# A streamed mixture of experts with its weights in 4 MB transfers and four slots instead of 2 MB transfers and eight

## The reference

```python
h = rmsnorm(x);  proj = h @ w_in            # 2048 x 5376
y = concat(rg_lru(...), short_conv(...), stick_breaking_attention(...))
x = x + (per_head_rmsnorm(y) * mix_norm) @ w_out      # 2048 x 2048
h2 = rmsnorm(x)
# group = argmax of 4 logits, then the top 2 of the group's 8 experts
for e in the token's two experts:           # w_gate, w_up: 32 x 2048 x 512
    hid = silu(h2 @ w_gate[e]) * (h2 @ w_up[e])
    x = x + gate_e * (hid @ w_down[e])      # w_down: 32 x 512 x 2048
```

## Time and profile before

| | us |
|---|---|
| median of 3 runs | 1350.33 |
| lowest and highest | 1348.47, 1351.5 |
| span of the profiled execution | 1347.2 |
| the profiled execution's own time | not recorded apart from its span |

### The profile page before, as it was taken

How to read it: one execution, slowest core, us unless ns; L and a number is a source line. 1 busy time by engine, 2 the same in 40 slices (tenths; PEclk the granted TensorE clock), 3 DMA queues, 4 the chain that set the end, 5 groups by cost and what they waited for, 6 DMA issues and landing times.

```text
span 1347.2 us, 20449 instructions
## 1 busy us (share of the span) xinstructions
PE 1132.6 (84%) x8602; PEld 760.2 (56%) x8602; DVE 412.2 (31%) x700; ACT 308.0 (23%) x534; POOL 51.0 (4%) x64
## 2 busy tenths in 40 slices
PE   8999999999999878769778966976796697779676
PEld 7999999999985445226333522633352252335223
DVE  6545666675443333003101300300130030013002
ACT  6445576684430100000000000000100000010000
POOL 1110011501000000000000000000000000000000
PEclk9999999999999888779776877977887798779768
DMA  9954554745668999999999999999999999999995
GB/s 314 283 187 139 174 166 148 243 133 185 254 248 323 423 422 421 419 420 420 424 423 423 423 423 420 420 422 423 423 423 423 422 418 420 422 425 422 423 422 236
DMA packets 120306, 471.64 MB, mean 350 GB/s; under 512 B 8547, under 2 KB 69569, under 8 KB 103361
## 3 DMA queue, kind: packets, MB, share of 16 engines
q1 hardware_dynamic: 120256, 470.94, 87.8%
HBM read 468.83 MB, written 2.10 MB: 350 GB/s over the span
## 4 chain that ended last, share of the span: by engine, by line
PE 48%; DMA 41%; SPq 5%; DVE 2%; ACT 2%; issue 1%; DVEq 0%; ACTq 0%
PE bank L1316 24%; DMA ring<-in_w_up 22%; DMA ring<-in_w_down 14%; PE bank L1531 6%; DMA ring<-in_w_gate 5%; SPq L372 5%; PE bank L1482 5%; PE bank L1495 4%; PE bank L1563 3%; PE bank L1546 3%; PE bank L1268 1%; PE bank L1335 1%; DMA x_acc<-in_x 1%; PE bank L1367 0%; PE bank L1439 0%
## 5 line engine op out<-in xcount | busy, mean ns | idle before, releaser
L1531 PE MATMUL bank<-ring,x_exp 128*32 128x512 f32 x2048 | 298.3, 720 | 151.5 <-DMA ring<-in_w_up 104.8
L1531 PEld LDWEIGHTS bank<-ring,x_exp 128*32 128x32 f32 x2048 | 63.0, 121 | 356.3 <-DMA ring<-in_w_up 152.1
L865 DVE TENSOR_TENSOR w_lo<-ring,w_hi 128x1024 fp32r<-128x1024 f32 x116 | 145.4, 1271 | 141.5 <-ACT w_hi L549 141.4
L1563 PE MATMUL bank<-ring,hidT 128*32 128x256 f32 x2048 | 169.9, 501 | 22.0 <-DVE hidT L1223 21.2
L1316 PE MATMUL bank<-hT_hi,w_hi 128*128 128x256 f32 x576 | 164.7, 286 | 1.8 <-DVE hT_lo L836 1.8
L1316 PE MATMUL bank<-hT_hi,w_lo 128*128 128x256 f32 x576 | 163.0, 283 | 0.0
L1316 PE MATMUL bank<-hT_lo,w_hi 128*128 128x256 f32 x576 | 163.0, 283 | 0.0
L549 ACT ACTIVATE w_hi<-ring 128x1024 fp32r<-128x1024 f32 x116 | 121.8, 1059 | 134.7 <-PE bank L1316 134.7
L1218 DVE COPY up_sb<-bank 128x512 f32<-128x512 f32 x32 | 22.1, 692 | 396.2 <-PE bank L1531 396.2
L1563 PEld LDWEIGHTS bank<-ring,hidT 128*32 128x32 f32 x2048 | 84.5, 143 | 96.2 <-issue 77.2
L1316 PEld LDWEIGHTS bank<-hT_hi,w_hi 128*128 128x128 f32 x576 | 110.5, 192 | 2.2 <-issue 2.0
(11 more groups left out here) (229 smaller groups left out, 1163.2 us busy)
## 6 DMA issues: line engine op xcount, KB each, us to landing
ring<-in_w_gate SPq DMA_DIRECT2D x64, 2048.0 KB, 27.3
ring<-in_w_up SPq DMA_DIRECT2D x64, 2048.0 KB, 25.0
ring<-in_w_down SPq DMA_DIRECT2D x64, 2048.0 KB, 34.6
ring<-in_w_in SPq DMA_DIRECT2D x21, 2048.0 KB, 9.1
ring<-in_w_out SPq DMA_DIRECT2D x8, 2048.0 KB, 8.3
x_acc<-in_x SPq DMA_DIRECT2D x4, 1024.0 KB, 8.6
out<-x_acc SPq DMA_DIRECT2D x8, 256.0 KB, 2.2
lru_w<-in_lru_wa SPq DMA_DIRECT2D x1, 384.0 KB, 3.8
```

The costliest lines, as they stand in the source:

```text
L865: dve.tensor_tensor(w_lo[:, k].rearrange("p c n -> p (c n)"), src, w_hi[:, k].rearrange("p c n -> p (c n)").bitcast(F32), ALU.subtract).th ...
L1531: ins = pe.matmul(dst[SLOTS * j:SLOTS * (j + 1), :], x_exp[:, c, cols], weights[:, cc * F:(cc + 1) * F], start=(c < 4), stop=(c >= KC - 4))
L1563: ins = pe.matmul(b_down[h][SLOTS * n:SLOTS * (n + 1), 0:DB], hidT[:, f, :], weights[:, f * (D // 2) + n * DB:f * (D // 2) + (n + 1) * DB] ...
```

## The change

- `PARTS` goes from 6 to 3: whole gate, whole up, whole down, one transfer of 4 MB each. Every one is a single run of 32 KB in each partition.
- The experts' ring is `twin`, four slots of 4 MB over the same memory, in the order of old slots 6+7, 2+3, 0+1, 4+5. Its semaphores are its own. Each slot is released when the whole matrix is used.
- TensorE multiplies a whole matrix between two waits. The number of gate and up matmuls is the same; down is 16 matmuls with 512 columns instead of 32 with 256.
- The down product needs one bank. It is copied out once after the whole of it, 512 columns in each copy, and `combine` waits for that.
- Quad 0 gathers all four blocks and transposes the gates ahead of its first item, as the other quads do.

```diff
@@ -55,7 +55,7 @@
 
     PW = 256
     PIECE = KC * PW * 4
-    MIX_RING, MOE_RING = 4, 8
+    MIX_RING, MOE_RING = 4, 4
 
     BLK_XA, BLK_GA, BLK_BG = 0, HA, 2 * HA
     BLK_CG, BLK_XB = BLK_BG + HB, BLK_BG + 2 * HB
@@ -72,14 +72,13 @@
     Y_ORDER = (3, 0, 1, 2)
 
 
...
     QI = 4
     QUADS = NE // QI
     XQ = 4
     NX = XQ * QI
     NI = NE + NX + QI
-    H = KC // 2
 
     x_t = x[0].rearrange("(t p) d -> t p d", p=P)
     out_t = out[0].rearrange("(t p) d -> t p d", p=P)
@@ -104,7 +103,8 @@
         w_lo = at("w_lo", [4, 4, PW], F32R, 5 * PIECE)
 
         ring_at = [i * PIECE for i in range(6)] + [o_proj + 16 * SEQ * 4 + i * PIECE for i in range(2)]
-        ring = [at(f"ring{i}", [KC * PW], F32, ring_at[i]) for i in range(MOE_RING)]
+        ring = [at(f"ring{i}", [KC * PW], F32, ring_at[i]) for i in range(MIX_RING)]
+        twin = [at(f"twin{i}", [2 * KC * PW], F32, ring_at[i]) for i in (6, 2, 0, 4)]
         o = 6 * PIECE
         x_acc = at("x_acc", [TILES, D], F32, o)
...
@@ -198,13 +198,14 @@
         AUX = 4
 
         b_gate, b_up, b_fold = bank[0], bank[1], bank[2]
-        b_down = [bank[3], bank[4]]
+        b_down = bank[3]
         b_gath, b_comb = [bank[4], bank[5]], [bank[6], bank[7]]
 
 
         x_in, par_in, router_in = [sem(f"x_in{t}") for t in range(TILES)], sem("par_in"), sem("router_in")
         lru_in, x_again, out_done = sem("lru_in"), sem("x_again"), sem("out_done")
...
@@ -248,25 +249,21 @@
         give_full, give_ready = sem("give_full"), sem("give_ready")
 
 
-        MOE_ORDER = [6, 7] + [(N_MIX + i) % MIX_RING for i in range(MIX_RING)] + [4, 5]
-        MIX_USES = [len(range(i, N_MIX, MIX_RING)) for i in range(MIX_RING)] + [0] * 4
         PER_QUAD = PARTS * QI
         assert PER_QUAD % MOE_RING == 0
 
         def place_of(k, i):
 
-            return MOE_ORDER[(PARTS * k + i) % MOE_RING]
+            return (PARTS * k + i) % MOE_RING
 
         def piece_count(q, k, i):
 
-            rounds = (PARTS * k + i) // MOE_RING + 1 + MIX_USES[place_of(k, i)]
+            rounds = (PARTS * k + i) // MOE_RING + 1
             return q * (16 * PER_QUAD // MOE_RING) + 16 * rounds
 
 
         def piece_source(i, e):
-            if i < 4:
-                return (w_gate_p, w_up_p)[i % 2][e][:, (i // 2) * H:(i // 2 + 1) * H, :]
-            return w_down_p[e][:, :, (i - 4) * (D // 2):(i - 3) * (D // 2)]
+            return (w_gate_p, w_up_p, w_down_p)[i][e]
 
         def out_block(b):
 
...
@@ -355,13 +352,13 @@
                 def item_pieces(k, e):
                     for i in range(PARTS):
                         m = PARTS * k + i
-                        if isinstance(q, int) and m < 2:
+                        if isinstance(q, int) and m == 0:
 
                             sp.wait_ge(y_split, 4)
-                        elif isinstance(q, int) and m < 6:
-
-                            sp.wait_ge(lo_ready, 4 * (N_MIX - 6 + m) + 4)
-                        elif isinstance(q, int) and m < 8:
+                        elif isinstance(q, int) and m < 3:
+
+                            sp.wait_ge(lo_ready, 4 * (N_MIX - 3 + m) + 4)
+                        elif isinstance(q, int) and m == 3:
 
                             sp.wait_ge(quarter_used, 4 * N_MIX)
                         else:
@@ -369,8 +366,8 @@
                             sp.wait_ge(piece_used, q * PER_QUAD + (m - MOE_RING + 1))
                         place = place_of(k, i)
                         src = piece_source(i, e)
-                        sp.dma_start(ring[place][:, :].rearrange("p (c n) -> p c n", n=src.shape[2]),
-                                     src).then_inc(piece_in[place], 16)
+                        sp.dma_start(twin[place][:, :].rearrange("p (c n) -> p c n", n=src.shape[2]),
+                                     src).then_inc(twin_in[place], 16)
 
                 for k in range(QI):
...
@@ -746,7 +743,7 @@
             def item_step(q, k):
                 i = q * QI + k
 
-                act.wait_ge(piece_used, i * PARTS + 3)
+                act.wait_ge(piece_used, i * PARTS + 1)
                 if not (isinstance(q, int) and i == 0):
                     act.wait_ge(fold_full, i)
                 act.activation(gate_sb[:, :], b_gate[:, :], ACT.Copy).then_inc(gate_out, 1)
@@ -757,11 +754,10 @@
                 act.activation(silu_sb[:, :, :], b_fold[:, 0:P].rearrange("p (f s) -> p f s", f=FC),
                                ACT.Silu).then_inc(silu_ready, 1)
 
-                for h in range(2):
-                    act.wait_ge(piece_used, i * PARTS + (5 + h))
-                    for n in range(2):
-                        ins = act.activation(y_cols(k, h, n), b_down[h][SLOTS * n:SLOTS * (n + 1), 0:DB], ACT.Copy)
-                    ins.then_inc(y_out_act, 1)
+                act.wait_ge(piece_used, i * PARTS + 3)
+                for n in range(2):
+                    ins = act.activation(y_cols(k, n), b_down[SLOTS * n:SLOTS * (n + 1), :], ACT.Copy)
+                ins.then_inc(y_out_act, 1)
 
             def quad(q, n_extra=None):
...
@@ -1194,7 +1190,7 @@
                 for b in range(4):
                     dve.wait_ge(gath_full, q * 4 + (b + 1))
                     if not isinstance(q, int) and b == 0:
-                        dve.wait_ge(piece_used, q * PER_QUAD - 2)
+                        dve.wait_ge(piece_used, q * PER_QUAD - 1)
                     dve.tensor_tensor(x_exp[:, 4 * b:4 * b + 4, :],
                                       b_gath[b % 2][:, :].rearrange("p (c s) -> p c s", c=4),
...
@@ -1224,11 +1220,10 @@
                                   b_fold[:, P:2 * P].rearrange("p (f s) -> p f s", f=FC),
                                   ALU.mult).then_inc(hid_ready, 1)
 
-                for h in range(2):
-                    dve.wait_ge(piece_used, i * PARTS + (5 + h))
-                    for n in range(2, 4):
-                        ins = dve.tensor_copy(y_cols(k, h, n), b_down[h][SLOTS * n:SLOTS * (n + 1), 0:DB])
-                    ins.then_inc(y_out_dve, 1)
+                dve.wait_ge(piece_used, i * PARTS + 3)
+                for n in range(2, 4):
...
@@ -1467,10 +1462,10 @@
             keep_clock(bank[0], 10)
 
 
-            def outputs_written(q, k, h):
-
-                pe.wait_ge(y_out_act, q * (2 * QI) + (2 * k + h + 1))
-                pe.wait_ge(y_out_dve, q * (2 * QI) + (2 * k + h + 1))
+            def outputs_written(i):
+
...
@@ -1512,24 +1507,19 @@
                 first = isinstance(q, int) and i == 0
                 cols = slice(SLOTS * k, SLOTS * (k + 1))
 
-                for p in range(4):
-                    if first and p == 2:
-
-                        gather(q, range(2, 4))
-                        transpose_gates(q)
-                    weights = ring[place_of(k, p)]
-                    pe.wait_ge(piece_in[place_of(k, p)], piece_count(q, k, p))
-                    dst = (b_gate, b_up)[p % 2]
-                    if p < 2 and not first:
+                for p in range(2):
+                    weights = twin[place_of(k, p)]
+                    pe.wait_ge(twin_in[place_of(k, p)], piece_count(q, k, p))
+                    dst = (b_gate, b_up)[p]
+                    if not first:
                         pe.wait_ge((gate_out, up_out)[p], i)
-                    for cc in range(H):
-                        c = (p // 2) * H + cc
+                    for c in range(KC):
                         j = c % 4
-                        if k == 0 and p % 2 == 0 and j == 0:
+                        if k == 0 and p == 0 and j == 0:
 
                             pe.wait_ge(gath_out, q * 4 + (c // 4 + 1))
                         ins = pe.matmul(dst[SLOTS * j:SLOTS * (j + 1), :], x_exp[:, c, cols],
-                                        weights[:, cc * F:(cc + 1) * F], start=(c < 4), stop=(c >= KC - 4))
+                                        weights[:, c * F:(c + 1) * F], start=(c < 4), stop=(c >= KC - 4))
                     ins.then_inc(piece_used, 1)
                 if k == QI - 1:
                     keep_clock(bank[5], 5)
@@ -1551,33 +1541,26 @@
                     keep_clock(bank[5], 6)
 
                 pe.wait_ge(hid_ready, i + 1)
-                for h in range(2):
-                    if not first:
-
-                        pe.wait_ge(y_out_act, q * (2 * QI) + (2 * k + h - 1))
-                        pe.wait_ge(y_out_dve, q * (2 * QI) + (2 * k + h - 1))
-                    weights = ring[place_of(k, 4 + h)]
-                    pe.wait_ge(piece_in[place_of(k, 4 + h)], piece_count(q, k, 4 + h))
-                    for f in range(FC):
-                        for n in range(4):
-                            ins = pe.matmul(b_down[h][SLOTS * n:SLOTS * (n + 1), 0:DB], hidT[:, f, :],
-                                            weights[:, f * (D // 2) + n * DB:f * (D // 2) + (n + 1) * DB],
-                                            start=(f == 0), stop=(f == FC - 1))
-                    ins.then_inc(piece_used, 1)
```

(30 more changed lines are left out.)

11 lines of the change are left out of this document (7 added, 4 removed).

## The result

| | before | changed |
|---|---|---|
| median, us | 1349.49 (4 runs, 1348.47 to 1351.50) | 1338.83 (4 runs, 1338.73 to 1339.32) |
| span of the profiled execution | 1347.2 | 1337.0 |
| mean granted clock | 0.875 | 0.883 |

What follows compares the result with a forecast made beforehand. The prediction took transfers to bound the experts' stage. Run length -18.7, start +5.8 and end +5.0 sum to -7.9 us, from 1350.33 to 1342.4, with a range of 1336 to 1352.

Steps and rivals of the forecast that it cites:

- What bounds the kernel: Experts' stage: transfers set the pace (DMA share 1.01 at 422 GB/s) and TensorE follows; the mixer's stage is TensorE's.
- Run length: Experts' stream: fewer, longer runs bring every 4 MB matrix to 9.73 us; over 91 matrices -18.7 us.
- The start: First refill: it waits for the whole gather and all of gate, so it goes out later, +5.8 us.
- The end: After the last up lands: more matmuls on up, partly at lower clock, and `combine` waiting for copies, +5.0 us.
- Hidden work: Other items and quad boundaries: later releases cost nothing; worst release 36.7 us after up's landing, 10 us to spare.
- The rival of a dry ring: Between quads: the ring empties if TensorE is 10 us later than worked out; +30 us, 1372; chance 0.05.
- gate and up gain nothing: Gate and up transfers: no gain from longer runs, down only reaches their pace; -1.5 us, 1348.8; chance 0.17.
- down is slow for its place: Down's transfers: slow for following up while TensorE folds, so pace stays; +10.8 us, 1361; chance 0.05.
- its weaker form: Down's transfers: two fifths of the extra are its runs', the rest its place; +3.3 us, 1353.6; chance 0.08.

Runs made afterwards that it cites:

- down16: Kernel before, with each down piece cut by rows, one run of 16 KB instead of four of 4 KB: median 1336.86 us, ratio 0.9888.
- runs16: Changed kernel with two of its four slots split into two 16 KB stretches, still one transfer per matrix: median 1342.84 us, ratio 0.9933.
- two_dmas: Changed kernel with each matrix fetched by two transfers of 2 MB (16 KB runs): median 1345.78 us, ratio 0.9953.
- cols: Changed kernel with the down product in halves of the columns, each half copied out while the next is multiplied: median 1339.57 us, ratio 0.9913.
- best: Changed kernel with the edits of early, cols and up_half together: median 1332.95 us, ratio 0.9859.
- best2: best without the six idle matmuls between fold and down: median 1333.94 us, ratio 0.9878.
- late8: Changed kernel with 29 idle matmuls ahead of the gather of quads 1 to 7: median 1342.82 us (two executions), ratio 0.9935.
- again: The changed kernel itself, measured once more on the same chip as edits of its end: median 1339.92 us, ratio 0.9918.
- early: Changed kernel with the first item in halves as before and the two first refills cut in half: median 1335.0 us, ratio 0.9878.
- up_half: Changed kernel with the last up of each quad in two transfers of 2 MB: median 1336.37 us, ratio 0.9897.
- no_spin: Changed kernel without the six idle matmuls between fold and down of each quad's last item: median 1339.38 us, ratio 0.9916.

## Why the prediction held, step by step

**What bounds the kernel** held: in every run above the span ends 27 to 34 us after the last up has landed, so that this landing and the work behind it are the time.

**Run length** held. Down's excess goes with the way it is cut (down16), and going from 16 to 32 KB brings 9.5 ns a run (runs16, two_dmas) where 8.5 had been carried over from down. Beyond 16 KB the length of the runs is shown to be the cause, since runs16 changes nothing in the stream but that and where in a partition the halves lie. Between 4 and 16 KB the strided source is a second difference which no run takes away; that the two prices are nearly the same speaks for the runs there too. The forecast's 9.73 us was 9.715. By the traces the pace accounts for 30 x (10.21 - 9.715) + 61 x (9.80 - 9.715) = 20.0 us of the 22.1; the forecast had 18.7. The remaining 2 us are no pace. Of these 1.1 are in a stretch of the trace before, which the forecast read past, since it took its pace from 604.49 on and its stretch from 410.35. TensorE's timeline there is this:

```profile
573.59 3.64 PE L1531 MATMUL bank<-ring,x_exp 128*32 128x512 f32 x16 [1.27 <-DMA ring<-in_w_up]
...
589.94 1.92 PE L1531 MATMUL bank<-ring,x_exp 128*32 128x512 f32 x16 [0.70 <-DMA ring<-in_w_gate]
594.68 3.24 PE L1531 MATMUL bank<-ring,x_exp 128*32 128x512 f32 x16 [2.82 <-DMA ring<-in_w_up]
```

From the second half of up to the next item's first half are 21.09 us, where the same four pieces take 20.01 in the earlier trace rows. Another 0.4 us is lost between 453.94 and 469.45. The traces of cols, best, best2 and late8 have such losses of 1.0 to 2.7 us as well; those of the changed kernel, again, early, down16, two_dmas, runs16, up_half and no_spin have none above 0.3 us past 453 us. Over all their executions runs16 stays within 0.9 us, two_dmas within 1.4 and the changed kernel within 0.6 and later 1.6, the kernel before within 5.8. What causes these losses stays open, and so does whether the change has a part in their being rarer.

The Trainium skill's price of about 3 cycles per packet ("DMA: Bandwidth & Descriptors", "Why small descriptors are slow") would be 3.5 ns at the fabric clock that the Trainium skill gives there. The runs show 8.5 ns between 4 and 16 KB and 9.5 between 16 and 32 KB: it names the right cost and under a half of its size. The Trainium skill's fabric ceiling of 435 GB/s (same page, "Specifications") agrees: 4.194304 MB in 9.715 us are 432 GB/s, just below it.

**The start** held: 5.5 us for 5.8, and early takes all of it back.

**The end** was mis-sized, 6.3 us for 5.0. Of the parts, up at a clock between the two levels was right (5.15 us against the 1.92 of before, 3.2 for 3.5) and so nearly were the copies (1.8 for 1.5). What the sum left out is that the idle matmuls between fold and down can run at the lower clock as well (2.91 us for 12 records, 1.58 at full clock in up_half) and hold down back by 2.0 us, where it was 0.7. Also, the 26.9 us that it started from were an end at full clock: in the trace before, up, the idle matmuls and down were all granted 1.00. That the range of 3.3 to 6.8 holds the 6.3 is in part luck: in again the end costs 7.5 us, with up at 6.34 and down at 5.01, a term for which the sum had nothing. In down16 an end of 33.0 us stands behind a last up of half the size. So what the end costs depends on the clock at least as much as on the large slots; only up_half's medians, 2.5 to 3.6 us lower, show the slots' own part.

**Hidden work** held: 36.8 us to the release for 36.7, and about 9 us of room for 10. The forecast took one boundary for all of them, though; at the first the release comes after 42.8 us and the room is 2 to 3. The rival of a dry ring is real, but at the other boundaries it begins only where TensorE is 8 to 9 us later.

**The rivals.** That gate and up gain nothing is refuted by two_dmas and runs16. That down is slow for its place is refuted by down16, in its weaker form too: all of the 0.21 us a piece went.

The total was nearer than its parts. The stream gave 3.4 us more than forecast, the start cost 0.3 less and the end 1.3 more.

## What to carry to other kernels

A stream that is bound by its transfers gets faster with longer runs, and these do not need large slots: down16 had 15.4 of the stream's 22.1 us with the old ring, by cutting one matrix along the other axis, and its median was not above the changed kernel's. What large slots cost is paid once, where the ring is full before the consumer starts (the first release) and after the last landing (all of a large piece's work), and both can be had back by cutting only the transfers at these two places. Look for the room of a ring at every boundary, not at a typical one. Before counting on a saved wait near the end, look at which clock the work behind it would run at.

## What was not expected of the hardware

- The price of a run hardly falls with its length: 8.5 ns on an engine between 4 and 16 KB, 9.5 between 16 and 32 KB, where the mixer's rows had suggested 15 at 1 KB and a falling line.
- Idle matmuls about paid for themselves. Without six of them down began 2.0 us earlier and took 6.53 us, mostly at the lower of TensorE's two levels (1.2 and 2.4 GHz; granted 0.56), instead of 3.88 or, in the second trace of the changed kernel, 5.01.
- Issuing one transfer of 2 MB held SP for up to 15.84 us while down was cut in runs of 4 KB, and for no more than 0.35 us where all runs have 32 KB. The DMA share beside it was 1.01, so it did not starve the stream.
